# Window scores of the samples: high and low query parts share one stationary block, two products instead of three

## The reference, cut to what matters

```python
def _dil_sample(q, k, v, win_k, win_v):      # q, k, v: (8 samples, 8 tokens, 8 heads, 64)
    k_all = jnp.concatenate([win_k, k], axis=1)      # 2048 kept keys and 8 new ones
    v_all = jnp.concatenate([win_v, v], axis=1)
    for window, dil in ((128, 1), (512, 4), (2048, 16)):
        ...
        s = jnp.einsum("bthd,btkhd->bthk", q, kg).astype(jnp.float32) * DIL_SCALE
        p, lse = _softmax_lse(jnp.where(valid[None, :, None, :], s, NEG))
        outs.append(jnp.einsum("bthk,btkhd->bthd", p.astype(vg.dtype), vg))
    return _combine_dil(outs, lses)
```

## Time and profile before

| | us |
|---|---|
| Median of 3 runs | 1675.1 |
| The three runs | 1675.1, 1751.92, 1670.3 |
| Profiled execution, its own time | 1663.64 |
| Span of the profiled execution, first to last instruction | 1661.9 |
| Busy in the span: PE, DVE, ACT, POOL | 1586.6, 1157.3, 798.3, 925.5 |

### The profile page before, as it was taken

One profiled execution on the slowest core, in us unless ns is written; L12 is line 12 of the kernel. 1 busy time (PEld: TensorE's weight loads), 2 busy tenths in 40 slices (PEclk: granted clock), 3 DMA queues, 4 the chain that ended last, 5 costly groups with the idle time before them and its releaser, 6 DMA issues. The chain is left out here.

```text
span 1661.9 us, 29386 instructions
## 1 busy us (share of the span) xinstructions
PE 1586.6 (95%) x10057; PEld 1422.9 (86%) x10057; DVE 1157.3 (70%) x2017; ACT 798.3 (48%) x1692; POOL 925.5 (56%) x909
## 2 busy tenths in 40 slices
PE   7999999999998999999899799999999999999997
PEld 6788888888887888888778699999999999888876
DVE  6533337888786886878634976656666666798896
ACT  5322226878677776777522443333333333433354
POOL 1000006667674897988501797767777775344464
PEclk9999999999999999999999899999999999999999
DMA  8367644432344776656566166656666665965532
GB/s 280 126 171 238 223 148 108 115 101 55 105 116 119 198 206 177 178 155 198 172 203 197 60 178 187 210 168 181 195 187 215 176 199 200 356 215 165 181 116 91
DMA packets 218098, 285.37 MB, mean 172 GB/s; under 512 B 35929, under 2 KB 140506, under 8 KB 212780
## 3 DMA queue, kind: packets, MB, share of 16 engines
q1 hardware_dynamic: 217954, 283.53, 56.2%
HBM read 235.92 MB, written 114.67 MB: 211 GB/s over the span
## 5 line engine op out<-in xcount | busy, mean ns | idle before, releaser
L2817 POOL TENSOR_TENSOR lead<-acc,lead 128x512 fp32r<-128x512 f32 x110 | 147.2, 1347 | 107.1 <-ACT lead L2949 107.0
L832 PE MATMUL zp<-win_h,xT_h 128*128 128x512 f32 (+1 forms) x288 | 113.1, 393 | 3.3 <-DVE acc L681 3.3
L1222 POOL TENSOR_SCALAR a_pr<-a_pr,a_rden 128x256 f32<-128x256 f32 (+7 forms) x128 | 95.4, 757 | 32.4 <-DVE a_rden L1332 32.3
L2949 ACT CAST lead<-acc 128x512 fp32r<-128x512 f32 x105 | 64.9, 620 | 99.2 <-PE z_ps L3475 58.8
L832 PE MATMUL zp<-win_l,xT_h 128*128 128x512 f32 (+1 forms) x288 | 111.9, 389 | 0.0
L3007 ACT CAST lead<-d_ring 128x512 fp32r<-128x512 f32 x73 | 45.4, 622 | 127.2 <-PE r_ps L3567 33.3
L1270 ACT ACTIVATE a_pr<-a_pr,a_nm 128x256 f32<-128x256 f32 (+7 forms) x128 | 98.5, 773 | 10.6 <-DVE a_nm L1326 10.0
L832 PE MATMUL zp<-win_h,xT_l 128*128 128x512 f32 (+1 forms) x256 | 99.5, 388 | 0.0
L2888 POOL TENSOR_TENSOR u_op<-d_w,u_op 128x512 fp32r<-128x512 f32 x39 | 53.6, 1379 | 77.1 <-ACT u_op L3019 77.1
L1412 PE MATMUL a_o<-a_pp,a_vv 128*128 128x256 f32 x576 | 85.9, 294 | 4.8 <-DVE a_pp L1336 4.8
L2817 POOL TENSOR_TENSOR u_op<-acc,u_op 128x512 fp32r<-128x512 f32 x44 | 80.3, 1827 | 8.9 <-ACT u_op L3045 8.9
(11 more groups left out here) (443 smaller groups left out, 5351.5 us busy)
## 6 DMA issues: line engine op xcount, KB each, us to landing
out_s_win_k<-in_state_win_k SPq DMA_DIRECT2D x40, 816.0 KB
out_s_win_v<-in_state_win_v SPq DMA_DIRECT2D x40, 816.0 KB
d_ring<-scratch_s_a SPq DMA_DIRECT2D x106, 256.0 KB, 3.1
acc<-in_state_win_k SPq DMA_DIRECT2D x16, 768.0 KB, 6.1
acc<-in_state_win_v SPq DMA_DIRECT2D x16, 768.0 KB, 6.1
scratch_s_a<-u_us SPq DMA_DIRECT2D x22, 544.0 KB, 6.2
acc<-in_w_gate SPq DMA_DIRECT2D x23, 512.0 KB, 9.3
acc<-in_w_up SPq DMA_DIRECT2D x22, 512.0 KB, 11.6
```

Of the source, the lines that this page charges most:

```text
L832: last = nc.tensor.matmul(z[:, 0:n], a, b, start=(k == 0 and i == 0), stop=(k == KC - 1 and i == len(terms) - 1))
L1222: nc.gpsimd.tensor_scalar(p, p, self.rden[:, k % 2, h:h + 1], 1.0, ALU.mult, ALU.mult)\
L2817: nc.gpsimd.tensor_tensor(op[n][:, 1, :], src, op[n][:, 0, :].bitcast(F32), ALU.subtract).then_inc(S["lo"], 1)
L2949: copy(op[n][:, 0, :], src).then_inc(S["hi"], 1)
```

## The change

The block of the high queries and that of the low ones become one, `w_qb`. The half of the 128 stationary columns that held zeros now holds the low parts. Two matmuls by high keys and low keys then give high queries by both key parts in one half of `w_s_ps`, and low queries by both key parts in the other half. ACT copies the low half's 64 rows to `w_low` in SBUF, in the 64 partitions of the other half. DVE adds `w_s_ps` and that copy into `w_low`, and the custom instruction takes `w_low` as its input where it took `w_s_ps`. PE's wait before a new unit is on the addition (`s_sum`). The planner's costs of `score` and the window side's share of the stage change too.

```diff
-        self.qb_h, self.qb_l = ([sb(f"w_qb{n}{i}", [P, i * NS + PAIRS * STEP], F32R) for i in range(2)] for n in "hl")
+        self.qb = [sb(f"w_qb{i}", [P, NS + PAIRS * STEP], F32R) for i in range(2)]
+        self.low = sb("w_low", [P, 512])
...
# work
-            return {"tensor": matmuls(3, w)} | ({"vector": 0.00148 * w} if e[1] % 4 == 3 else {})
+            sums = {"scalar": 0.05 + 0.00094 * w, "vector": 0.1 + 0.0025 * w}
+            return {"tensor": matmuls(2, w)} | (sums if e[1] % 4 == 3 else {})
...
# after
-            return {"tensor": need, "vector": [x("tensor", *e), x("sync", "const"), x("tensor", "p_turn", b // 12 - 2, 1)]}
+            return {"tensor": need, "scalar": [x("tensor", *e), x("vector", "score", b - 4)],
+                    "vector": [x("scalar", *e), x("sync", "const"), x("tensor", "p_turn", b // 12 - 2, 1)]}
...
# gpsimd, setup
-            for a in (*self.qb_h, *self.qb_l):
+            for a in self.qb:
                 nc.gpsimd.memset(a[:].bitcast(F32), 0.0).then_inc(S["pads"], 1)
...
# scalar
-            for qb, qT in ((self.qb_h[b % 2], self.qT_h), (self.qb_l[b % 2], self.qT_l)):
-                block = qb[:, b % 2 * NS:].rearrange("p (i n) -> p i n", i=PAIRS)
+            for half, qT in ((b % 2, self.qT_h), (1 - b % 2, self.qT_l)):
+                block = self.qb[b % 2][:, half * NS:half * NS + PAIRS * STEP].rearrange("p (i n) -> p i n", i=PAIRS)
...
+        elif e[0] == "score":
+            g = e[1]
+            b, j = divmod(g, 12)
+            if j % 4 == 3:
+                w = sum(self.KEYS[j // 4])
+                act.wait_ge(S["s_ps"], g + 1)
+                if g > 4:
+                    act.wait_ge(S["s_free"], g // 4)
+                nc.scalar.copy(self.low[self.half(b), 0:w], self.SC[self.half(b + 1), 0:w]).then_inc(S["s_low"], 1)
...
# vector
-            dve.wait_ge(S["s_ps"], g + 1)
+            dve.wait_ge(S["s_low"], g // 4 + 1)
...
+            nc.vector.tensor_tensor(self.low[rows, 0:w], self.SC[rows, 0:w], self.low[rows, 0:w], ALU.add).then_inc(S["s_sum"], 1)
+            dve.wait_ge(S["s_sum"], g // 4 + 1)
...
-                out=self.pr[rows, cols], in0=self.SC[rows, 0:w], in1=self.window[rows, cols], scale=-DIL_SCALE,
+                out=self.pr[rows, cols], in0=self.low[rows, 0:w], in1=self.window[rows, cols], scale=-DIL_SCALE,
...
# tensor
-                pe.wait_ge(S["s_free"], 3 * b + u)
+                pe.wait_ge(S["s_sum"], 3 * b + u)
...
-            qh, ql = self.qb_h[b % 2], self.qb_l[b % 2]
-            for n, (a, k) in enumerate(((qh, self.kT_h), (qh, self.kT_l), (ql, self.kT_h))):
-                last = nc.tensor.matmul(self.SC[:, 0:w], a[:, x], k[g % 2][:, 0:w], start=(i == 0 and n == 0),
-                                        stop=(i == PAIRS - 1 and n == 2))
+            for n, k in enumerate((self.kT_h, self.kT_l)):
+                last = nc.tensor.matmul(self.SC[:, 0:w], self.qb[b % 2][:, x], k[g % 2][:, 0:w], start=(i == 0 and n == 0),
+                                        stop=(i == PAIRS - 1 and n == 1))
...
# attention, second stage
-            run(own, ring, sides, ((0, 1), (0.02, 0.92)))
+            run(own, ring, sides, ((0, 1), (0.03, 0.93)))
```

More of the change, by code:

```diff
@@ L2065, in __init__ @@
             "const q_in k_new0 v_in0 v_in1 v_new0 v_new1 pads neg_go turn_go "
-            "qb s_ps s_free exp recip v_hi v_ok o_ps o_ok").split()}
+            "qb s_ps s_low s_sum s_free exp recip v_hi v_ok o_ps o_ok").split()}
         self.S["stored"] = io["sems"].keep("w_stored")
@@ L2269, in scalar @@
             if b == 0:
-                act.wait_ge(S["pads"], 4)
+                act.wait_ge(S["pads"], 2)
                 self.ring.done(act, ("pre",))
```

## The result

The changed kernel takes 1681.53 us (median of 6 runs, 1677.23 to 1683.45); the six runs of before beside it have a median of 1666.87. One of the six, 1751.92, is a slow execution and does not enter the ratio. The ratio is 1.0095, with a 95% interval of 1.0067 to 1.0123: about 16 us slower, where 4 us faster was forecast. By the 2% bound it is no change, but it is clear of the noise.

The account below looks back on a forecast made before the run. PE was the fullest engine, with DVE taking its place: 227.5 + 14.4 + 15.6 = 257.5 us of DVE work over 0.89 gives a 289.3 us stage, 4.1 less, so 1659.5, carried to 1668; range 1650 to 1684.

Parts of the forecast that it names:

- ACT's copy: 24 copies out of PSUM in the stage, 12.4 us on ACT, taken as hidden at 0; upper end 6 us.
- the hold: Reductions with both inputs in SBUF stand until POOL's current instruction ends: 0.65 us each, 15.6 us on DVE, ends 0 and 25.
- Matmuls removed: In the changed stage, 96 matmuls of high keys by low queries go, saving 18.2 us on PE by start spacing.
- the sum's division by 0.89: Stage length taken as DVE's 257.5 us of work over 0.89, its highest share found: 289.3 us against 293.4.
- The addition: 24 new DVE instructions in the stage, 8 for each width, at 0.553, 0.561 and 0.685 us: 14.4 us.
- DVE's own wait between addition and reduction: DVE's wait on `s_sum` before each reduction, put at nothing because the reduction waited on DVE's earlier one before too.
- rival C: Slower: POOL holds the 24 reductions over 0.8 us each; 1679, up to 1685 with the longer way to a new unit; chance 0.20.
- Rival B: PE's 18.2 us pass in full, reductions slipping between POOL's instructions: -18 to -25 us, time 1647 to 1655; chance 0.25.
- The base: The 9 us carried from the profiled execution's 1663.6 us to the median of the runs, making 1659.5 into 1668.
- The zeros: Two stage terms taken as 0: ACT's copy (up to 6 us) and PE's longer wait at a new unit (up to 11).
- the moved share: The window side's share moves by 1% of the stage, 2.9 us; put at 0, costing up to 2.9.
- Rival D: PE idles more and one more gap like 649 to 655 comes, with half clock: 6.9 us, time 1675; chance 0.10.

## Why the prediction was wrong, point by point

**Where the 16 us come from.** One ladder in one order, by ratio: old instructions in the new order +7.3; less the third matmul, +1.7, so the cut gives 5.6; with ACT's copy and DVE's addition, +9.8, so these cost 8.1; with the reduction held by POOL, +15.8, so the hold costs 6.0. The first step is clear of its interval (±4 us), and so is what the added work costs in all, from +1.7 to +15.8, 14 us (some ±7). The cut and the hold, as steps of this ladder, are no larger than their uncertainty (±6 to 7 us). The cut was clear of noise in the old order (5.3 us), the hold in the order of the other share (18 us), so the sizes are this order's and not constants.

**Matmuls removed: the count was right, what they are worth was not.** 192 scores are left. The forecast let PE's 18.2 us pass in full as far as DVE had room. With the order held, the cut alone passed 5.3 and 5.6 us, and putting the matmul back in the changed kernel cost 9; with its own plan the cut passed nothing.

**The step that failed** is the sum's division by 0.89: that the stage is as long as DVE's work over the highest share that one stretch of 20 us had shown. DVE's work was forecast well (257.5 us, measured 253.3), but it stood at 0.82. With the sum in PSUM, DVE's 242.0 us should have made a stage of 272 us by that rule, and made 301.5. And for the cut alone, with DVE's 227 us, the rule gives 256 us and lets PE's 18.2 pass in full; with the order held 5 to 9 us passed. The 0.89 was itself no ceiling: it is the highest value on one grid of stretches, and 10 us further on in the kernel before, with PE at 0.95, DVE is at 19.41 of 20 us, 0.97:

```profile
540.50:560.50 20.00, 19.01 (x129) 15.32 (x128) 19.41 (x51) 15.34 (x35) 17.99 (x20) 1.00 0.86 239
```

With 0.97 the same sum would have forecast a stage of 265 us, farther still from the 309.4. So DVE's load does not set the length, and a share taken from the best 20 us was not kept by the whole stage in any variant. What fits the runs is waits between engines that go through fixed lists: the order alone moved the time with the instructions unchanged. Which waits, and how far the two buffers of the keys and the five banks of the ring have a part in them, was not tried; that stays open.

**The terms.** The addition: 14.4 us forecast, 14.4 measured. DVE's own wait between addition and reduction, put at nothing, came to up to 5.1 us: the idle time ahead of the three groups of reductions is 1.7 us each, and 3.4 of the 5.1 are put down to the addition. The hold: 0.65 us for each reduction, 15.6 in all, measured (27.9 - 15.4) / 24 = 0.52, or 12.5; so the estimate from POOL's rows was near. With both inputs in SBUF the reduction was held (mean 1.16 us), with one in PSUM it was not (0.64 before). The Trainium skill, "SBUF — State Buffer", section "Who interferes with whom", has the rule that a DVE instruction with two SBUF inputs contends with a GpSimd instruction that reads SBUF; the trace agrees. I gave rival C this mechanism. The sign of the result is C's, and the ratio puts it at about 16 us over before where C had 6.4 to 12.4 (1679 to 1685 less the median of 1672.6 that stood behind them). But C's cause is only some 6 us of it; that C's time came near is in part luck. Rival B, the full 18.2 us, did not come even without the added instructions. The base was too high as well: I carried 9 us from the profiled execution to the median, and the six runs of before are 3.2 us over it; the forecast gain of 4 us does not depend on that.

**The zeros.** PE's wait for the addition did cost nothing (0.2 us, once). ACT's copy came out at 12.3 us (4.7 + 3.8 + 3.8). Whether it alone is hidden was not tried apart from the addition: copy and addition together cost 8.1 us by the ladder. With PE adding, where ACT keeps its copy, nothing is lost against before. That would fit DVE's addition as the dear part, but the order differs there too, so it is not shown.

**The order.** I set the moved share at 0 and up to 2.9 us, and did not price the new order at all. It was worth 7.3 us in the changed plan, 7.5 between the two plans for the cut, 20 for the changed kernel with the share moved back, and 19 with the old costs. That is the term that was missing, and each of these is more than the forecast's whole gain.

**The clock.** Rival D had one more gap; there were four more stretches at half clock in the profiled executions, 17 us more in all, of which at most half, 8.5 us, is lost. The executions of one and the same kernel say what the clock goes with. In the 25 of before that stand beside the cut in the new order and PE's addition, the mean clock of the execution lies between 0.973 and 0.985 and the time between 1677.2 and 1655.8 us: 1.6 us slower for each 0.001 less (correlation -0.93). The six of the changed kernel have a mean of 0.976, these 25 of 0.979. By that slope some 4 us of the 16 go with the clock (an estimate) and most of the difference does not. The rows of one such case in the changed kernel (PE alone, in order of time):

```profile
730.48 0.60 PE L1393 MATMUL l_bank<-ident_sb,a_pr 128*128 128x128 f32 x4
732.59 0.56 PE L2397 MATMUL l_bank<-ident_sb,acc 104*128 104x104 f32 x4 [1.51 <-DVE a_kh L1301]
734.88 1.12 PE L1393 MATMUL l_bank<-ident_sb,a_pr 128*128 128x128 f32 x4 [1.73 <-DVE w_pt L2318]
```

Two waits for DVE of 1.5 and 1.7 us come close together, and from 735 to 739 the clock is 0.50, its lower level. This is an account and no experiment: no run changed the clock alone. The slowest variants have the most such time (54.7 us with the old costs, 47.7 with the share back) and the fastest have little (10.2 with PE's addition, 17.1 for the cut in the old order). But PE's addition with the share to 0.91 also has 10.2 us, and a stage of 295.0.

## What to carry to other kernels

When a planner writes each engine's list, an edit changes two things, the instructions and the order. Measure each without the other before you believe either: here the order alone moved the time by 7 to 20 us, more than the edit's own gain. In a stage like this one, where several engines stand at 70 to 95% and hand work round, work removed from the fullest one was worth three tenths to a half of its length, and the work added (26.9 us on DVE, 12.3 on ACT) cost 14 us, about half of DVE's. Before you move a DVE input from PSUM to SBUF, look whether the other one lies in SBUF and what GpSimd does at that time.

## What the runs showed of the hardware that was not expected

The hold works both ways: POOL's copy of 1.05 us took 1.35 beside a held reduction, and with the same instructions in the same order POOL was busy for 251.8 us with the reductions held and for 244.5 without. And in the profiled executions the order alone, with the same instructions, took the time at half clock in the stage from 13.6 to 27.3 us.
